# The query stage of a two-block kernel: raw tiles and a division by the norm afterwards

## The chip, the cores and the metric

The kernel runs on one core of one Trainium2 chip. The metric is the device time of one execution in microseconds, measured on the same chip for both kernels; a profiled execution has a time of its own. An engine is a queue of instructions that runs in its own order: TensorE (products, PE in the profile), VectorE (DVE), ScalarE (ACT), GpSimd (POOL, here only DMA issue) and SyncE (SP, here only the loads of the weight stream).

## The reference, cut to what matters

Two transformer blocks over 256 tokens of width 1024 in float32. The first has two layers (sparse attention, a short convolution, an MLP). The second has one layer: two kinds of attention, then a retrieval of experts by product keys. The change touches the step between them, in these lines:

```python
def rms_norm(x, g):
    xf = x.astype(jnp.float32)
    y = xf * lax.rsqrt(jnp.mean(xf * xf, axis=-1, keepdims=True) + EPS)
    return (y * g.astype(jnp.float32)).astype(x.dtype)

def modulate(h, shift, scale):
    return h * (1.0 + scale[:, None, :]) + shift[:, None, :]

        x = x + gate1[:, None, :] * (mixed @ w_out[layer])
        h2 = modulate(rms_norm(x, norm2_g[layer]), shift2, scale2)
        x = x + gate2[:, None, :] * peer(h2, w_query[layer], sub_keys[layer],
                                          u_experts[layer], v_experts[layer])

    # in peer, for the tokens xc of h2:
        qh = (xc @ w_query).reshape(PEER_CHUNK, PEER_HEADS, PEER_QDIM)
        s1 = jnp.einsum('thd,hnd->thn', qh[..., :PEER_HALF], sub_keys[:, 0]).astype(jnp.float32)
        s2 = jnp.einsum('thd,hnd->thn', qh[..., PEER_HALF:], sub_keys[:, 1]).astype(jnp.float32)
        # top 16 of each, top 16 of their sums, softmax, then u and v of the chosen experts
```

For one token, h2 = r * (a * x) + shift2, where r is one number of the token (the reciprocal root of its mean square) and a = gain * (1 + scale2) and shift2 are vectors over the 1024 features. So a query is r * ((a * x) @ w_query) + shift2 @ w_query. The expert stage, which follows, needs h2 itself.

## The kernel before, in words

**Weights.** All weights come as one stream of pieces of [128, 1024] float32, 512 KB each, in the order of use, through a ring of four slots (`RING`). A piece is split in two numbers, w_hi (ScalarE, `split_hi`, line 185) and w_lo (VectorE, `split_lo`, line 190). Each product is then three TensorE instructions (`mm3`, lines 213 to 215): hi by hi, lo by hi, hi by lo. `next_piece` starts each piece, and first issues the split of the piece three ahead (`AHEAD`): w_hi waits until that piece has landed and until the slot's old piece has been used, w_lo waits for w_hi, the load of the next piece into the raw slot (SyncE, line 563) waits for w_lo. `piece_b` runs one piece of 8 feature tiles against the 256 tokens: 24 products of 256 columns. TensorE waits in `next_piece` for w_lo of its piece.

**Marks.** `PE`, `AC` and `VE` are helpers (class `Line`) for the queues of TensorE, ScalarE and VectorE: `VE.go(marks, method, ...)` waits for the marks, issues the instruction (line 88) and returns its mark. Each engine runs strictly what was written for it, in the order of the Python program, so an instruction that waits holds all behind it on its engine. `free[b]` holds the marks after which PSUM bank b may be written again, and `take(b)` waits for them on TensorE.

**Before the query stage.** The output product of the attention (`out_part`) fills banks 0 to 3: 2 token tiles (tt) by 2 column halves (n). `add_out(tt, n)` multiplies a bank by the gate and adds it to x, two VectorE instructions; `square_of` squares the chunk on ScalarE and sums it. `token_roots` makes the reciprocal root of each token by a chain of 15 small VectorE instructions, `diagonals` puts the roots on the diagonals of two 128x128 matrices. `keep_clock` issues products whose result nobody reads. `modulated_to_u` multiplies x by the diagonals on TensorE (line 1169), which turns and divides it in one step (32 products), and then makes the eight feature tiles of h2: scale and shift to hT, alternately on ScalarE and VectorE, u_hi on ScalarE, u_lo on VectorE.

**The query stage.** 16 pieces of w_query. The first two run tile by tile as the tiles become ready (`two_pieces`, lines 229 to 241), the other 14 in pairs through `piece_b`, each pair in a half of one bank (4, 5 or 6); ScalarE copies them to qhT, which lies in the big buffer Z. `key_scores(h)` makes 8 small products (line 1576) of the queries 2h and 2h + 1 with the sub-keys, and VectorE copies them out. The last three come together at the end. Then the expert stages start: 256 pieces, the first 64 beside the choice of the experts, which is VectorE's. x is written to memory (x_parked) before Z takes its place.

**Layer boundary.** Between the two layers of the first block the same thing is done in another way: `added_and_turned` turns x undivided (line 366), lowers the eight tiles with the gain alone, and the root is applied later.

Of the kernel before, what the change touches and what calls it, by code (L numbers as in the profile page):

```python
# [8 lines left out]
F32 = mybir.dt.float32  # L9
# [8 lines left out]
P = 128  # L18
# [31 lines left out]
U_SHIFT, U_REST = 56, 8  # L50
N_LAYER = 59 + 2 * KH
# [42 lines left out]
def build(nc, stream, x_in, gains2, gain_cols, conv_w, w_ada, b_ada, c_cols, kept_in, rope_in, na_mask_in,  # L94
          t5_in, t5_hot, rpb_pad, sinks, sub_keys, gain_out, out):
    ctx = ExitStack()
    with ctx:
        def sb(c, name, shape, dt=F32):
            return c.enter_context(nc.sbuf_tensor(name, shape, dt))
# [117 lines left out]
        def piece_b(o, rhs_hi, rhs_lo, kt=KD, parts=1, last=False, ready=None):  # L217

            s = next_piece(last)
            for part in range(parts):  # L220
                for k in range(kt):
                    if ready is not None:
                        PE.wait(*ready[k])
                    col = (part * kt + k) * P
                    i = mm3(o[part], w_hi[:, s, col:col + P], w_lo[:, s, col:col + P],
                            rhs_hi[:, k, :], rhs_lo[:, k, :], k == 0, k == kt - 1)
            return used(i)
# [292 lines left out]
        ph1a = ph1.enter_context(ExitStack())  # L520
        rope_t = sb(ph1a, "rope", [P, 2, T])
# [4 lines left out]
        gate = sb(ph1a, "gate", [P, 2 * KD, T])  # L526
# [10 lines left out]
        o_hi, o_lo = sb(ph1a, "o_hi", [P, KW, T], F32R), sb(ph1a, "o_lo", [P, KW, T], F32R)  # L537
        y_hi, y_lo = sb(ph1a, "y_hi", [P, KW, T], F32R), sb(ph1a, "y_lo", [P, KW, T], F32R)
# [545 lines left out]
        bias_a, bias_b = sb(ph1b, "bias_a", [P, H, BIAS_W]), sb(ph1b, "bias_b", [P, H, BIAS_W])  # L1084
        na_mask = sb(ph1b, "na_mask", [P, GRID_W])
        sink = sb(ph1b, "sink", [P, H])
# [6 lines left out]
        og, junk = sb(ph1b, "og", [P, 2, W]), sb(ph1b, "junk", [P, 2, W])  # L1093

# [53 lines left out]
        def diagonals(r):  # L1148
            for tt in range(NT):
                m = VE.go((r, (s_kept, 16)), V.tensor_scalar, diag[:, tt, :], ident, st[:, 3, tt:tt + 1], None, ALU.mult)  # L1150
                got["diag", tt] = m

# [352 lines left out]
        square_of(x, 5, x_marks, 0, 1)  # L1505
        PE.wait(*got["mixed", 1, 1])
# [6 lines left out]
        split_lo(c + KW)  # L1513
        for n in range(2):
# [25 lines left out]
        qhT = Z[:, 0:N_QUERY * T].rearrange("p (f t) -> p f t", t=T)  # L1540
        skT = Z[:, N_QUERY * T:N_QUERY * (T + PK)].rearrange("p (f n) -> p f n", n=PK)
# [17 lines left out]
        AC.wait((s_park, 16))  # L1559
        VE.wait((s_park, 16))  # L1560
        take(4), take(5)
        pair = two_pieces([bank[4][:, 0:T], bank[5][:, 0:T]], h2_ready)
        for f in range(2):
            m = AC.go((pair[f],), S.activation, qhT[:, f, :], bank[4 + f][:, 0:T], ACT.Copy)
            free[4 + f] = (m,)
        S.dma_start(skT, sub_keys).then_inc(s_sk, 16)
        q_there = [m]

        def key_scores(h):
# [3 lines left out]
            PE.wait(q_there[h], (s_sk, 16))  # L1573
# [9 lines left out]
        for f in range(2, N_QUERY, 2):  # L1583
            b = 4 + (f // 2) % 2 if f > 2 else 6
            take(b)
            piece_b([bank[b][:, 0:T]], *U)
# [4 lines left out]
            q_there.append(m)  # L1591
            if 2 < f < N_QUERY - 2:
                key_scores(f // 2 - 2)
        key_scores(PH - 3)
        key_scores(PH - 2)
        m = key_scores(PH - 1)
# [485 lines left out]
```

## Time and profile before

| | us |
|---|---|
| median of 3 runs | 1728.52 |
| lowest and highest | 1727.76, 1728.98 |
| the profiled execution's own time | 1727.02 |
| its span | 1725.7 |
| TensorE busy | 1700.7 (99%) |
| VectorE busy | 1328.3 (77%) |
| ScalarE busy | 926.5 (54%) |

The place of the change lies at 877 to 939 us of the span. The mean granted clock of TensorE over the span is 0.997 of full speed. A TensorE row shows when a product was issued; its duration is longer than the distance to the next, because products are pipelined, so costs are read from start to start. Rows of VectorE and ScalarE overlap by about 0.1 us with their neighbours when nothing is waited for.

### The profile page before, as it was taken

What the parts mean: (1) busy time and instruction counts of PE and PEld (TensorE: products, weight loads), DVE (VectorE), ACT (ScalarE), POOL (GpSimd) and SP (SyncE); (2) the same over time, 40 slices, a digit from 0 to 9 for tenths busy, and PEclk for the clock granted to TensorE, in tenths of its full rate; (3) what the DMA queues carried; (4) which work ended last, traced back from release to release, by engine and by line L of the source; (5) the groups of instructions that cost most, each with busy time, mean ns of one, the idle gap of its engine ahead of it and who ended that gap; (6) DMA issues with size and microseconds to landing.
All of it is one profiled execution on the core that took longest, in us unless ns stands there. A gap on an engine that the chain in (4) does not pass through costs nothing.

```text
span 1725.7 us, 33390 instructions
## 1 busy us (share of the span) xinstructions
PE 1700.7 (99%) x11670; PEld 1567.1 (91%) x11670; DVE 1328.3 (77%) x2382; ACT 926.5 (54%) x1647; POOL 63.3 (4%) x112
## 2 busy tenths in 40 slices
PE   9999999999999999999999999999999999999997
PEld 8899899989999899999889999999999988888886
DVE  7986778778976788877775999978888766666666
ACT  5454544455454544455554555577777655444553
POOL 0000001000000122100000000000000000000000
PEclk9999999999999999999999999999999999999999
DMA  6555687755445699744344555554444455555554
GB/s 233 174 187 205 209 294 270 250 174 171 159 160 168 221 329 327 238 153 140 123 167 152 173 170 179 182 171 141 141 138 144 141 191 193 194 194 194 191 192 152
DMA packets 90122, 327.30 MB, mean 190 GB/s; under 512 B 11000, under 2 KB 11176, under 8 KB 89584
## 3 DMA queue, kind: packets, MB, share of 16 engines
q1 hardware_dynamic: 79056, 286.45, 48.8%
q0 software_dynamic: 9712, 34.36, 6.0%
q10 hardware_dynamic: 1264, 5.24, 0.8%
q8 instruction: 62, 1.02, 0.2%
q14 instruction: 28, 0.23, 0.0%
HBM read 323.88 MB, written 6.09 MB: 191 GB/s over the span
## 4 chain that ended last, share of the span: by engine, by line
PE 80%; DVE 16%; issue 2%; ACT 1%; DMA 0%; DVEq 0%; ACTq 0%
PE bank L213 24%; PE bank L215 24%; PE bank L214 24%; DVE Z L88 6%; DVE w_lo L190 5%; PE bank L1772 3%; PE bank L284 1%; DVE yc L88 1%; PE bank L276 1%; PE bank L1313 1%; PE bank L484 1%; DVE work L88 1%; DVE rot L88 1%; DVE top L88 1%; PE bank L1264 0%
## 5 line engine op out<-in xcount | busy, mean ns | idle before, releaser
L190 DVE TENSOR_TENSOR w_lo<-raw,w_hi 128x1024 fp32r<-128x1024 f32 x544 | 658.0, 1220 | 154.1 <-ACT w_hi L185 153.3
L185 ACT ACTIVATE w_hi<-raw 128x1024 fp32r<-128x1024 f32 x544 | 572.5, 1054 | 229.2 <-PE bank L215 162.4
L213 PE MATMUL bank<-u_hi,w_hi 128*128 128x256 f32 x2400 | 686.2, 286 | 3.7 <-DVE w_lo L190 3.0
L214 PE MATMUL bank<-u_lo,w_hi 128*128 128x256 f32 x2400 | 674.7, 281 | 0.0
L215 PE MATMUL bank<-u_hi,w_lo 128*128 128x256 f32 x2400 | 674.7, 281 | 0.0
L213 PEld LDWEIGHTS bank<-u_hi,w_hi 128*128 128x128 f32 x2400 | 453.0, 189 | 12.8 <-DVE w_lo L190 4.3
L214 PEld LDWEIGHTS bank<-u_lo,w_hi 128*128 128x128 f32 x2400 | 453.2, 189 | 2.3
L215 PEld LDWEIGHTS bank<-u_hi,w_lo 128*128 128x128 f32 x2400 | 452.9, 189 | 0.0
L215 PE MATMUL bank<-w_hi,a_lo 128*128 128x512 f32 x744 | 290.6, 391 | 0.0
L214 PE MATMUL bank<-w_lo,a_hi 128*128 128x512 f32 x744 | 290.4, 390 | 0.0
L213 PE MATMUL bank<-w_hi,a_hi 128*128 128x512 f32 x744 | 289.9, 390 | 0.0
L215 PEld LDWEIGHTS bank<-w_hi,a_lo 128*128 128x128 f32 x744 | 139.6, 188 | 29.4
L213 PEld LDWEIGHTS bank<-w_hi,a_hi 128*128 128x128 f32 x744 | 139.9, 188 | 27.9 <-issue 0.2
L214 PEld LDWEIGHTS bank<-w_lo,a_hi 128*128 128x128 f32 x744 | 139.6, 188 | 28.1
L1861 ACT ACTIVATE a_hi<-Z 128x256 fp32r (+1 forms) x126 | 52.7, 418 | 169.0 <-PE bank L215 167.2
L1863 DVE TENSOR_TENSOR a_lo<-Z,a_hi 128x256 fp32r<-128x256 f32 x126 | 53.6, 425 | 81.6 <-ACT a_hi L1861 81.6
L1761 ACT ACTIVATE rows_a<-rows_a,sel 128x128 f32<-128x128 f32 x256 | 81.2, 391 | 0.0
L1745 DVE TENSOR_TENSOR rows_a<-kept,sel 128x512 f32<-128x512 f32 x64 | 44.2, 691 | 34.5 <-PE bank L1772 34.5
L962 ACT ACTIVATE qT<-bank 128x256 f32<-128x256 f32 x64 | 24.6, 384 | 82.5 <-PE bank L215 82.3
L1608 ACT ACTIVATE Z<-bank 128x256 f32 (+1 forms) x68 | 26.1, 384 | 76.8 <-PE bank L215 76.7
L971 DVE CAST a_hi<-qT 128x256 fp32r<-128x256 f32 x60 | 18.1, 301 | 48.4 <-PE bank L215 47.3
L997 DVE SCALAR_TENSOR_TENSOR space<-gate,c_tmp,space 128x1024 f32 x42 | 53.7, 1280 | 0.4
(286 smaller groups left out, 1710.6 us busy)
## 6 DMA issues: line engine op xcount, KB each, us to landing
raw<-stream SPq DMA_DIRECT2D x544, 512.0 KB, 3.3
gate<-w_ada POOLq DMA_DIRECT2D x48, 512.0 KB, 6.0
t_rows<-t_by_distance POOLq DMA_DIRECT2D x8, 256.0 KB, 3.1
rpb_rows<-rpb_pad POOLq DMA_DIRECT2D x8, 224.0 KB, 4.1
bias_b<-rpb_rows POOLq DMA_DIRECT2D x16, 96.0 KB, 6.3
bias_a<-t_rows POOLq DMA_DIRECT2D x1, 1536.0 KB, 13.1
x<-x_in ACTq DMA_DIRECT2D x2, 512.0 KB, 5.5
gains_b<-gains POOLq DMA_DIRECT2D x1, 1024.0 KB, 8.7
```

Source lines behind the costliest of these rows:

```text
L88: return self.done(method(*args, **kw))
L185: nc.scalar.activation(w_hi[:, s, :], raw[:, s, :], ACT.Copy).then_inc(s_hi, 1)
L190: nc.vector.tensor_tensor(w_lo[:, s, :], raw[:, s, :], w_hi[:, s, :].bitcast(F32), ALU.subtract).then_inc(s_split, 1)
L213: M.matmul(o, lh, rh, start=start, stop=False, skip_group_check=True)
L214: M.matmul(o, lh, rl, start=False, stop=False, skip_group_check=True)
L215: return M.matmul(o, ll, rh, start=False, stop=stop, skip_group_check=True)
L997: nc.vector.scalar_tensor_tensor(total, ada_raw[:, k % ADA_RING, :], c_act[:, k:k + 1], total, ALU.mult, ALU.add).then_inc(s_ada, 1)
L1745: return V.tensor_tensor(out, iota.unsqueeze(1).to_broadcast([P, GROUP, P]), values.unsqueeze(2).to_broadcast([P, GROUP, P]), ALU.is_equal)
L1761: i = S.activation(rows_a[:, q, e, :], rows_a[:, q, e, :], ACT.Copy, scale=share[:, e:e + 1])
L1772: i = M.matmul(bank[6 + q][:, e * P:(e + 1) * P], rows_a[:, q, e, :], rows_b[q][:, e, :].bitcast(F32), start=True, stop=True, skip_group_c ...
L1861: S.activation(hi[:, q, :], zj, ACT.Copy).then_inc(s_ah, 1)
L1863: V.tensor_tensor(lo[:, q, :], zj, hi[:, q, :].bitcast(F32), ALU.subtract).then_inc(s_al, 1)
```

## The change

The tiles of a * x (`raw_u_hi`, `raw_u_lo`) are made from x before its norm is known, as at the layer boundary, with two columns more: both hold shift2, so that a product of 258 columns gives the query of all tokens and, in column 256, shift2 @ w_query. The first ten query pieces run on these. Each result is then multiplied by a row of the roots (`token_row`, made by two small products with the diagonals) and the shift's part is added. x is turned by plain transposes, eight of them between the halves of the last output products, with each pair of feature tiles in one of the banks 4 to 7. The eight tiles of h2 are made from the same banks by `tile_fixed`, between the steps of pieces 6 to 9. Pieces 10 to 15 run on h2 as before. The filler products, the scaling products, `two_pieces` and `modulated_to_u` are not used here any more. The squares of the last two chunks and the waits for the parking of x move behind; the bias tables give their place to the raw tiles.

```diff
         def piece_b(o, rhs_hi, rhs_lo, kt=KD, parts=1, last=False, ready=None, order=None):
             s = next_piece(last)
+            order = order or tuple(range(kt))
             for part in range(parts):
-                for k in range(kt):
+                for k in order:
...
+        def turn_tile(k, tt, marks, turned):
+            b, col = turn_place(k)          # bank 4 + k // 2, half k % 2
+            if tt == 0 and k % 2 == 0:
+                take(b)
+            PE.wait(marks[tt][k // 4], (s_kept, 16))
+            i = M.transpose(bank[b][:, col + tt * P:col + (tt + 1) * P], x[:, tt, k * P:(k + 1) * P], ident)
+            if tt == NT - 1:
+                turned[k] = PE.done(i)
+
+        def shift_columns(hi, lo, j, scaled):
+            src = acol[:, 2 * j, :].unsqueeze(2).to_broadcast([P, KD, 2])
+            m1 = AC.go((scaled,), S.activation, hi[:, :, T:T + 2], src, ACT.Copy)
+            return m1, VE.go((m1, scaled), V.tensor_tensor, lo[:, :, T:T + 2], src, hi[:, :, T:T + 2].bitcast(F32),
+                             ALU.subtract)
+
+        LOWER_ORDER = (0, 2, 1, 3, 4, 6, 5, 7)
+
+        def lower_scaled(k, hi, lo, j, scaled, turned):
+            b, col = turn_place(k)
+            src, gain, t = bank[b][:, col:col + T], acol[:, 2 * j + 1, k:k + 1], turned[k | 1]
+            m1 = AC.go((t, scaled, *(free[b] if k % 2 else ())), S.activation, hi[:, k, 0:T], src, ACT.Copy, scale=gain)
+            m = VE.go((m1, t, scaled), V.scalar_tensor_tensor, lo[:, k, 0:T], src, gain, hi[:, k, 0:T].bitcast(F32),
+                      ALU.mult, ALU.subtract)
+            free[b] = (m1, m)
+            return m1, m
+
+        def roots_as_row(b):
+            take(b)
+            PE.wait(got["diag", 0], got["diag", 1])
+            for tt in range(NT):
+                i = M.matmul(bank[b][:, tt * P:(tt + 1) * P], one[:, 0:1].to_broadcast([P, P]), diag[:, tt, :],
+                             start=True, stop=True, skip_group_check=True)
+            m = AC.go((PE.done(i),), S.activation, token_row[:, :], bank[b][:, 0:T], ACT.Copy)
+            free[b] = (m,)
+            return m
+
+        def rooted_and_shifted(b, dst, n, done, row):
+            m1 = AC.go((done,), S.activation, side_sum[:, n:n + 1], bank[b][:, T:T + 1], ACT.Copy)
+            m = VE.go((done, row, m1), V.tensor_tensor, dst, bank[b][:, 0:T], token_row[:, :], ALU.mult)
+            free[b] = (m, m1)
+            return AC.go((m, m1), S.activation, dst, dst, ACT.Identity, bias=side_sum[:, n:n + 1])
...
         split_hi(c + KW)
         split_lo(c + KW)
+        for k in range(KD):
+            turn_tile(k, 0, x_marks, turned2)
         for n in range(2):
...
             add_out(1, n)
+        for k in range(KD):
+            turn_tile(k, 1, x_marks, turned2)
+        raw_ready = {k: lower_scaled(k, *raw2, 1, scaled, turned2) for k in LOWER_ORDER}
+        split_lo(c + KW + 1)
+        split(c + KW + 2)
+        for n in range(2):
             square_of(x, 5, x_marks, 1, n)
-        take(5)
-        keep_clock(5, 20)
         diagonals(token_roots(junk_mark[0]))
-        split_lo(c + KW + 1)
         S.dma_start(x_dram.rearrange("t p d -> p t d"), x[:, :, :]).then_inc(s_park, 16)
-        split_hi(c + KW + 2)
-        h2_ready = modulated_to_u(x, x_marks, scaled, 1, 1)
-        split_lo(c + KW + 2)
...
+        def raw_query(f, b):
+            take(b)
+            return piece_b([bank[b][:, 0:T + 2]], *RAW2, ready=raw_ready if f == 0 else None,
+                           order=LOWER_ORDER if f == 0 else None)
+
+        def query_fixed(f, b, m):
+            q_there[f] = rooted_and_shifted(b, qhT[:, f, :], f, m, row)
+
+        def tile_fixed(k):
+            b, col = turn_place(k)
+            src, h = bank[b][:, col:col + T], hT[:, k % 4, :]
+            m = VE.go((row, turned2[k | 1]), V.scalar_tensor_tensor, h, src, acol[:, 3, k:k + 1], token_row[:, :],
+                      ALU.mult, ALU.mult)
+            free[b] = (m,)
+            m1 = AC.go((m,), S.activation, u_hi[:, k, :], h, ACT.Identity, bias=acol[:, 2, k:k + 1])
+            h2_ready[k] = (m1, VE.go((m, m1), V.scalar_tensor_tensor, u_lo[:, k, :], h, acol[:, 2, k:k + 1],
+                                     u_hi[:, k, :].bitcast(F32), ALU.add, ALU.subtract))
...
+        PE.wait(*shifts2)
+        m = raw_query(0, 0)
+        side_mark = AC.go((m,), S.activation, side_sum[:, 0:1], bank[0][:, T:T + 1], ACT.Copy)
+        first_there = AC.go((m,), S.activation, qhT[:, 0, :], bank[0][:, 0:T], ACT.Copy)
+        free[0] = (first_there,)
+        S.dma_start(skT, sub_keys).then_inc(s_sk, 16)
+        asked = {f: raw_query(f, f) for f in (1, 2)}
+        row = roots_as_row(3)
+        asked[3] = raw_query(3, 0)
+        m = VE.go((first_there, row), V.tensor_tensor, qhT[:, 0, :], qhT[:, 0, :], token_row[:, :], ALU.mult)
+        q_there[0] = AC.go((m, side_mark), S.activation, qhT[:, 0, :], qhT[:, 0, :], ACT.Identity,
+                           bias=side_sum[:, 0:1])
+        query_fixed(1, 1, asked[1])
+        asked[4] = raw_query(4, 3)
+        query_fixed(2, 2, asked[2])
+        query_fixed(3, 0, asked[3])
+        asked[5] = raw_query(5, 1)
+        query_fixed(4, 3, asked[4])
+        query_fixed(5, 1, asked[5])
+        asked[6] = raw_query(6, 2)
+        tile_fixed(0)
+        query_fixed(6, 2, asked[6])
+        asked[7] = raw_query(7, 3)
+        tile_fixed(1)
+        query_fixed(7, 3, asked[7])
+        key_scores(0)
+        asked[8] = raw_query(8, 2)
+        tile_fixed(2)
+        tile_fixed(3)
+        query_fixed(8, 2, asked[8])
+        key_scores(1)
+        asked[9] = raw_query(9, 3)
+        tile_fixed(4)
+        tile_fixed(5)
+        query_fixed(9, 3, asked[9])
+        tile_fixed(6)
+        tile_fixed(7)
+        for f in range(N_RAW, N_QUERY, 2):      # N_RAW = 10
+            b = 4 + (f // 2) % 2
             take(b)
-            piece_b([bank[b][:, 0:T]], *U)
+            piece_b([bank[b][:, 0:T]], *U, ready=h2_ready if f == N_RAW else None)
             m = piece_b([bank[b][:, T:2 * T]], *U)
...
+            key_scores(f // 2 - 3)
+        for h in range(PH - 3, PH):
+            m = key_scores(h)
+        AC.wait((s_park, 16))
+        VE.wait((s_park, 16))
```

## Rows read from the trace of the kernel before

**Rows 1.** The page, parts 1 and 4: busy time, and the chain by engine.
```profile
PE 1700.7 (99%) x11670; PEld 1567.1 (91%) x11670; DVE 1328.3 (77%) x2382; ACT 926.5 (54%) x1647; POOL 63.3 (4%) x112
PE 80%; DVE 16%; issue 2%; ACT 1%; DMA 0%; DVEq 0%; ACTq 0%
```

**Rows 2.** Timeline of TensorE, 876 to 887: start us, us, engine, line, operation, count, idle before.
```profile
877.44 0.39 PE L215 MATMUL bank<-w_hi,mx_lo 128*128 128x512 f32 x1
...
877.66 4.54 PE L276 MATMUL bank<-one_r 128*128 128x512 f32 x20
...
882.45 3.84 PE L1169 MATMUL bank<-space,x 128*128 128x128 f32 x32 [0.25 <-DVE space L88]
...
886.04 0.36 PE L213 MATMUL bank<-u_hi,w_hi 128*128 128x256 f32 x1
```

**Rows 3.** Busy time by stretch: us, each engine, PEclk, DMA share, GB/s.
```profile
910.00:936.00 26.00, 26.00 (x224) 26.00 (x224) 12.54 (x12) 10.35 (x12) 0.00 (x0) 1.00 0.48 163
```

**Rows 4.** Timeline of VectorE and ScalarE, 878 to 883.
```profile
878.59 0.69 DVE L88 TENSOR_TENSOR x<-x,hT 128x512 f32<-128x512 f32 x1
...
879.31 0.63 ACT L88 ACTIVATE space<-x 128x512 f32<-128x512 f32 x1 [0.67 <-DVE x L88]
...
880.07 0.16 DVE L88 SCALAR_TENSOR_TENSOR st<-st 128x2 f32<-128x2 f32 x1 [0.79 <-ACT space L88]
...
882.11 0.48 DVE L88 TENSOR_SCALAR space<-kept,st 128x128 f32<-128x128 f32 x2
```

**Rows 5.** Timeline, the first tile of h2: the three steps on two engines.
```profile
883.64 0.54 DVE L88 TENSOR_SCALAR hT<-bank,acol 128x256 f32<-128x256 f32 x1
884.21 0.42 ACT L88 ACTIVATE u_hi<-hT 128x256 fp32r<-128x256 f32 x1 [3.23 <-DVE hT L88]
...
884.73 0.43 DVE L88 TENSOR_TENSOR u_lo<-hT,u_hi 128x256 fp32r<-128x256 f32 x1 [0.55 <-ACT u_hi L88]
```

**Rows 6.** Timelines of TensorE, ScalarE and VectorE at the layer boundary, 383 to 388.
```profile
383.91 1.77 PE L366 MATMUL bank<-kept,x 128*128 128x128 f32 x12
...
384.22 3.02 ACT L88 ACTIVATE u_hi<-bank,kept 128x256 fp32r<-128x256 f32 x8 [1.51 <-PE bank L366]
...
384.78 3.21 DVE L88 SCALAR_TENSOR_TENSOR u_lo<-bank,kept,u_hi 128x256 fp32r<-128x256 f32 x8
```

**Rows 7.** Groups by form, whole span: count, busy us, mean ns, idle before.
```profile
L190 DVE TENSOR_TENSOR w_lo<-raw,w_hi 128x1024 fp32r<-128x1024 f32 x544 | 658.0, 1220 | 154.1 <-ACT w_hi L185 153.3 <-DVE Z L88 0.3
...
L965 DVE TENSOR_TENSOR qT<-qT,bank 128x256 f32<-128x256 f32 x64 | 26.5, 414 | 2.2 <-ACT qT L962 1.9
...
L88 DVE SCALAR_TENSOR_TENSOR u_lo<-bank,kept,u_hi 128x256 fp32r<-128x256 f32 x32 | 12.9, 475 | 0.0
...
L88 ACT ACTIVATE p<-p,rows 128x256 f32<-128x256 f32 x16 | 7.9, 496 | 1.1 <-DVE rows L88 1.1
```

**Rows 8.** Timeline of TensorE, the last pieces and key scores of the stage.
```profile
929.43 1.05 PE L1576 MATMUL bank<-Z 128*128 128x128 f32 x8
...
936.00 2.84 PE L1576 MATMUL bank<-Z 128*128 128x128 f32 x24
938.59 0.36 PE L213 MATMUL bank<-u_hi,w_hi 128*128 128x256 f32 x1
```

**Rows 9.** Timelines of VectorE and ScalarE, 890 to 900: splits of weights.
```profile
890.28 2.35 DVE L190 TENSOR_TENSOR w_lo<-raw,w_hi 128x1024 fp32r<-128x1024 f32 x2
...
895.65 1.06 ACT L185 ACTIVATE w_hi<-raw 128x1024 fp32r<-128x1024 f32 x1 [1.40 <-DMA raw<-stream]
...
899.42 1.06 ACT L185 ACTIVATE w_hi<-raw 128x1024 fp32r<-128x1024 f32 x1 [1.14 <-DMA raw<-stream]
```

**Rows 10.** Timeline of TensorE at 454, and busy time by stretch behind it.
```profile
453.99 0.72 PE L429 MATMUL bank<-kT,qT 64*128 64x128 f32 x8 [2.44 <-DVE qT L88]
...
455.00:457.00 2.00, 2.00 (x12) 2.00 (x11) 2.00 (x4) 0.00 (x0) 0.00 (x0) 0.50 0.33 106
457.00:459.00 2.00, 2.00 (x14) 2.00 (x13) 1.03 (x1) 0.00 (x0) 0.00 (x0) 0.66 0.90 289
```

More of the change, by code:

```diff
@@ L50 @@
 U_SHIFT, U_REST = 56, 8
+U_WIDE = T + 16
 N_LAYER = 59 + 2 * KH
@@ L215, in mm3, with piece_b @@
             return M.matmul(o, ll, rh, start=False, stop=stop, skip_group_check=True)
-        def piece_b(o, rhs_hi, rhs_lo, kt=KD, parts=1, last=False, ready=None):
+        def piece_b(o, rhs_hi, rhs_lo, kt=KD, parts=1, last=False, ready=None, order=None):
             s = next_piece(last)
+            order = order or tuple(range(kt))
             for part in range(parts):
-                for k in range(kt):
+                for k in order:
                     if ready is not None:
@@ L225, in piece_b @@
                     i = mm3(o[part], w_hi[:, s, col:col + P], w_lo[:, s, col:col + P],
-                            rhs_hi[:, k, :], rhs_lo[:, k, :], k == 0, k == kt - 1)
+                            rhs_hi[:, k, :], rhs_lo[:, k, :], k == order[0], k == order[-1])
             return used(i)
@@ L520, in build @@
         ph1a = ph1.enter_context(ExitStack())
+        gate = sb(ph1a, "gate", [P, 2 * KD, T])
+        o_hi, o_lo = sb(ph1a, "o_hi", [P, KW, T], F32R), sb(ph1a, "o_lo", [P, KW, T], F32R)
+        y_hi, y_lo = sb(ph1a, "y_hi", [P, KW, T], F32R), sb(ph1a, "y_lo", [P, KW, T], F32R)
         rope_t = sb(ph1a, "rope", [P, 2, T])
@@ L1093, in build @@
         og, junk = sb(ph1b, "og", [P, 2, W]), sb(ph1b, "junk", [P, 2, W])
+        token_row, side_sum = sb(ph1b, "token_row", [P, T]), sb(ph1b, "side_sum", [P, 3 * KD])
+        na_mask = sb(ph1b, "na_mask", [P, GRID_W])
+        sink = sb(ph1b, "sink", [P, H])
+        ph1c = ph1b.enter_context(ExitStack())
+        bias_a, bias_b = sb(ph1c, "bias_a", [P, H, BIAS_W]), sb(ph1c, "bias_b", [P, H, BIAS_W])
         G.wait_ge(s_naw, 16 * 8)
@@ L1505, in build @@
         square_of(x, 5, x_marks, 0, 1)
+        ph1c.close()
+        raw2 = [sb(ph1c, name, [P, KD, U_WIDE], F32R) for name in ("raw_u_hi", "raw_u_lo")]
+        shifts2 = shift_columns(*raw2, 1, scaled)
+        turned2 = {}
         PE.wait(*got["mixed", 1, 1])
@@ L1557, in build @@
         smx = tail(2 * NT * PH).rearrange("p (a n) -> p a n", a=2)
[L1559 to L1567, printed above, removed]
+        RAW2 = tuple(a[:, :, 0:T + 2] for a in raw2)
+        N_RAW = 10
+        U = (u_hi, u_lo)
+        q_there, h2_ready = {}, {}
+        def raw_query(f, b):
[13 more added lines that the diff above has]
+                                     u_hi[:, k, :].bitcast(F32), ALU.add, ALU.subtract))
         def key_scores(h):
@@ L1572, in key_scores @@
             take(b)
-            PE.wait(q_there[h], (s_sk, 16))
+            PE.wait(q_there[2 * h + 1], (s_sk, 16))
             for tt in range(NT):
@@ L1581, in key_scores @@
             return m
-        for f in range(2, N_QUERY, 2):
-            b = 4 + (f // 2) % 2 if f > 2 else 6
+        PE.wait(*shifts2)
[37 more added lines that the diff above has]
+            b = 4 + (f // 2) % 2
             take(b)
-            piece_b([bank[b][:, 0:T]], *U)
+            piece_b([bank[b][:, 0:T]], *U, ready=h2_ready if f == N_RAW else None)
             m = piece_b([bank[b][:, T:2 * T]], *U)
```

19 lines of the change are left out of this document (5 added, 14 removed).

## The prediction

> **What bounds the kernel now.** I read four views, in this order. The page first: TensorE is busy for 99% of the span, and it holds 80% of the chain that ended last [rows 1], so a change saves time only where it takes work or idle time off TensorE's queue. Then TensorE's timeline at the place of the edit. The last output product starts at 877.44 and the first query product at 886.04 [rows 2]. Between them lie only the 20 filler products and the 32 scaling products: 8.6 us in which the stream of useful products stands. Then the busy time by stretch: from 910 to 936 TensorE is busy for 26.00 of 26.00 us [rows 3], and the other engines show gaps. The expert stages behind are TensorE's as well, so what the query stage wins or loses arrives at the end unchanged. Last, the timelines of VectorE and ScalarE, which show what fills the 8.6 us: the add of the last chunk of x (878.59), the square (879.31), the root chain from 880.07, the two diagonals from 882.11 [rows 4], the scaling products, and the first tile (883.64 to 885.16) [rows 5].
>
> All times below are on the clock of that profiled execution: span 1725.7 us, its own time 1727.02. The median of the runs is 1728.52, so I add 1.5 us at the end.
>
> **The front: what is gained.** The root leaves the path to the first query product. Eight transposes go between the halves of the last output products. The trace has 12 in 1.77 us [rows 6] and 32 of the same size in 3.84 [rows 2], 0.12 to 0.15 each: 0.9 to 1.2 us, of which I take 0.9. The last output product then ends 0.9 later, and so does the second step of its add: 879.28 + 0.9 gives 880.15. The eight remaining transposes are two waits of four; the last four follow that add, 0.45 us. The lowering of a raw tile (ScalarE copy with gain, VectorE subtract) is the work of the layer boundary, where eight tiles took 3.02 and 3.21 us, 0.39 a tile [rows 6]. Here two tiles share a bank and the second must wait for VectorE's read of the first, so I count 0.46 a tile. VectorE runs 880.1 to 883.8, TensorE takes piece 0 behind it from 880.6 to 884.2.
>
> Piece 1 needs its w_lo, which now stands on VectorE behind the eight tiles: 883.7 + 1.22 [rows 7], start 885.0, a stall of 0.8. Then pieces 1 and 2 run to 890.7, two small products of the row of roots cost 0.25, and piece 3 starts at 890.95. Squares, roots, diagonals and w_lo of pieces 2 to 4 fill VectorE until 890.7 and are ahead of need. In the kernel before, a piece costs 2.85 (two pieces and a key score take 936.00 - 929.43 = 6.57, and three key scores 2.59, 0.86 each [rows 8]), so piece 3 started at 886.04 + 3 x 2.85 = 894.6. The front therefore gains 3.6 us and not 8.6: transposes and lowering take the rest. The columns added for the shift: a 512-column product is issued every 4.54/20 = 0.227 us [rows 2], a 256-column one every 2.85/24 = 0.119; by that slope two columns cost 0.9 ns, 240 of them 0.2 us. The trace shows no width between 256 and 512. Its bounds are nothing and the price of a 512-column product (a rival below).
>
> **The middle: what is lost.** From piece 3 on, the new work is written into the in-order queues of ScalarE and VectorE between the weight splits, and nearly every step waits for the other engine. Going through the queues in the order of the program: raw_query(f) first issues w_hi then w_lo of piece f + 3; then, for each query fixed, VectorE's multiply by token_row waits on ScalarE's one-column copy, and ScalarE's Identity waits on the multiply; for each tile, VectorE's multiply, ScalarE's u_hi, VectorE's u_lo, each waiting on the one before; and the next w_hi stands behind the last Identity. Prices:
> - split: 1.06 on ScalarE [rows 9], 1.22 on VectorE, less the overlap of neighbours (two w_lo in 2.35 [rows 9]): 2.2.
> - fixed query: multiply 0.41 [rows 7], Identity with a bias column from SBUF. This is not in the trace; nearest are the plain copy of the same size, 0.42 [rows 5], and the Exp with a bias column, 0.50 [rows 7]. I take 0.50, since it has the column. The one-column copy I put at 0.2 (0.42 for 256 columns and 0.63 for 512 [rows 4, 5] leave 0.21 at none); most of it lies beside w_lo. Together 0.95 to 1.0.
> - tile: multiply from PSUM 0.48 [rows 7], u_hi 0.50, u_lo 0.43 to 0.48, less 0.1 overlap plus two handoffs of 0.03 to 0.1 (884.18 to 884.21 and 884.63 to 884.73 [rows 5]): 1.4. The first tile of the kernel before took 1.52 for three such steps [rows 5].
>
> The Trainium skill (ScalarE: Activation LUTs, What ACT_TABLE_LOAD costs) says that each [128,1] pointer operand adds about 93 ns to an ACTIVATE. The 0.50 against 0.42 in the rows agrees; by the plain copy's price the sum below would be 1.4 us smaller.
>
> The chain begins with w_hi of piece 6. It waits for its raw tile, whose load starts when w_lo of piece 2 ends (886.0). At that time x_parked and sub_keys, 1 MB each, load too; in the kernel before, beside sub_keys alone, the loads started at 891.4 and 892.6 (w_lo until 892.63) were used at 895.65 and 899.42 [rows 9], 4.2 and 6.8 us later. I take 6.8: 892.9. With 4.2 or less, the row of roots (891.6) would decide, 1.3 earlier. From one w_hi to the next:
> - 6 to 7: split, first query fixed in two steps, query 1: 4.2 (897.1)
> - 7 to 8, 8 to 9: split and two queries, 4.2 each (905.5)
> - 9 to 10, 10 to 11: split, one tile, one query, 4.5 each (914.5)
> - 11 to 12: split, two tiles, one query, 6.0 (920.5)
> - 12 to the last u_lo: split, four tiles, one query, 8.45 (928.95)
>
> A piece costs TensorE 2.85, so it is held up throughout: piece 7 waits for bank 3 (query 4 fixed) until 903.9, piece 8 for bank 2 until 909.6, piece 9 for bank 3 until 914.1 and ends at 917.0. Piece 10 needs all eight tiles, and its last can start only at 929.0. TensorE stands for about 9.5 us there, and piece 10 ends at 929.35. Behind it: piece 11, a key score, four pieces with a key score between, four key scores, 5 x 2.85 + 6 x 0.86 = 19.4, to 948.8. Before, this point was 938.59 [rows 8]: 10.2 us later.
>
> **The clock.** After an idle stretch of 2.44 us at 451.5 to 453.99 the granted clock was 0.50 in 455 to 457 and 0.66 in 457 to 459, the lower level of 1.2 GHz [rows 10]: 2 x 0.50 + 2 x 0.34 = 1.7 us lost. In piece 10 the gaps between tiles are up to 4 us, and TensorE leaves it at the lower level; one such recovery then falls on the full stream of piece 11. I take 1.7, with 0 and 3.4 as ends. The shorter waits before pieces 7 to 9 may also cost clock, but there the two other engines decide, and it is hidden. The filler that is removed covered the 8.6 us; the new gap there is about 1.6 us, partly filled with transposes.
>
> Everything else I cost at nothing: x_parked is issued later, but waited for only behind the stage; the key scores of the first heads move later, and the copies of their results are counted as VectorE work beside ScalarE's; the two shift columns are made beside output products.
>
> **Sum:** 10.2 + 1.7 = 11.9 us later. 1727.02 + 11.9 = 1738.9, on the scale of the median 1740.4. Its own range: without clock loss, with the fast load and with the copy's price 11.9 - 1.7 - 1.3 - 1.4 = 7.5, so 1736; with 3.4 of clock and some 45 handoffs at 0.08 instead of 0.04, 11.9 + 1.7 + 1.8 = 15.4, so 1744.
>
> **Rivals.**
> - *The handoffs hide (not slower).* Counted by busy time alone, a raw piece asks 1.06 + 0.2 + 0.5 = 1.8 us of ScalarE and 1.22 + 0.41 = 1.6 of VectorE, less than 2.85, and VectorE's whole work from 889.5 on (nine w_lo, ten multiplies, sixteen tile steps, two copies of scores, 10.2 + 3.5 + 6.4 + 1.2 = 21.3 without waits) would end near 911. If the two run side by side, TensorE stays full to the end of piece 9 near 911, and only query 9 and the last two tiles (3.5 us against the 2.5 that piece 10 leaves them) hold it, 1.1. Then -3.6 + 0.2 + 1.1 = -2.3: 1726. For it: both engines show idle time. Against: the order of the queues, in which each step waits for the one just issued on the other engine. It decides wherever a split with its repairs takes under 2.85. Chance 0.11.
> - *The handoffs hide in part.* Queries keep up and only tiles 0 to 7 are serial, so the loss just eats the gain: within 3.5 us of before. 0.07.
> - *The raw products are slow.* 258 columns at the price of 512: 240 x 0.108 = 26 us more on TensorE, which takes over from the chain: piece 9 would end near 937 instead of 917, then 3.5 and 19.4 us, 961, or 22 us later: 1751. Nothing in the trace speaks for a step behind 256. 0.05.
> - *No clock loss*, or loads that land fast: 1737 to 1739, part of the forecast, which has 0.77 in all, near 0.7 of it in its own range.
>
> Faster, same and slower by 0.2% (3.5 us, about what these runs can tell from no change): the first rival gains 2.3 us and reaches 3.5 only with yet cheaper transposes: faster 0.06, same 0.12, slower 0.82. The range 1731 to 1744 leaves out the last rival, most of the first, and a little of the second.
>
> **What would show it.** First raw product at 880.6, piece 3 at about 891. A ladder in the timelines of ScalarE and VectorE in which one is idle while the other works, with w_hi every 4.2 us from 893, then 4.5 and 6. TensorE waiting for tiles in piece 10, the last at about 929, with the clock at 0.5. Products of 258 columns still 0.12 apart. The stage ending near 950. I am wrong if TensorE is full from 885 to 930, or if w_hi comes every 2.9.

## The result and the profile after

The changed kernel takes 1744.34 us (median of 4 runs, 1743.09 to 1745.18), the kernel before beside it 1728.75 (4 runs, 1727.76 to 1729.55). The ratio is 1.0091, 95% interval 1.0078 to 1.0104: 15.6 us slower. The forecast was 1740.4 with a range of 1731 to 1744: the sign and the ladder of handoffs were right, the size was 3.9 us short and lies just outside the range. The profiled execution of the changed kernel took 1744.12, its span 1742.8; its stage ends 16.8 us later than before, and its span is 17.1 longer. (That is more than 15.6, since the profiled execution of before lay 1.7 under its median and this one 0.2 under.)

TensorE's timeline, 872 to 893 (start, duration, engine, line, operation, count, idle before):

```profile
872.63 0.47 PE L214 MATMUL bank<-w_hi,mx_hi 128*128 128x512 f32 x1
...
875.50 1.03 PE L1166 MATMUL bank<-kept,x 128*128 128x128 f32 x8
876.29 0.48 PE L214 MATMUL bank<-w_hi,mx_hi 128*128 128x512 f32 x1
...
880.85 0.66 PE L1166 MATMUL bank<-kept,x 128*128 128x128 f32 x4 [0.75 <-DVE x L89]
881.34 0.36 PE L214 MATMUL bank<-raw_u_hi,w_hi 128*128 128x258 f32 x1
...
885.73 0.39 PE L214 MATMUL bank<-raw_u_hi,w_hi 128*128 128x258 f32 x1 [0.45 <-DVE w_lo L191]
...
891.59 0.61 PE L1194 MATMUL bank<-space,one 128*128 128x128 f32 x4
891.95 0.37 PE L214 MATMUL bank<-raw_u_hi,w_hi 128*128 128x258 f32 x1
892.15 0.28 PE L215 MATMUL bank<-raw_u_lo,w_hi 128*128 128x258 f32 x1
892.27 0.28 PE L216 MATMUL bank<-raw_u_hi,w_lo 128*128 128x258 f32 x1
```

This is the front, in place of the fillers and scaling products of [rows 2]. The first query product comes at 881.34 instead of 886.04, piece 1 stalls for 0.45 on its w_lo, and piece 3 starts at 891.95. Products of 258 columns are 0.12 apart, like those of 256. The row at 872.63 stands at 872.00 in the kernel before: this execution was 0.6 us late before any changed instruction.

The chain that ended last, 884 to 906 (start, duration, what). It leaves TensorE for the whole ladder (the row of w_hi steps up to piece 12 and the tiles behind it); over the span TensorE holds 76% of it, against 80% in [rows 1]:

```profile
884.54 2.28 DVE w_lo L191 x2
886.98 10.25 DMA raw<-stream
897.26 1.07 ACT w_hi L186
898.38 1.11 issue
899.49 0.43 DVE Z L89
899.94 0.51 ACT Z L89
900.61 0.44 DVE Z L89
901.09 0.39 issue
901.48 1.05 ACT w_hi L186
```

First a load of 10.25 us, then one step of the ladder in full: w_hi, w_lo, VectorE's multiply, ScalarE's Identity, the second multiply, the second Identity and the next w_hi. (The two "issue" rows are w_lo, on VectorE from 898.35 to 899.57, and the second Identity, on ScalarE from 901.07 to 901.58.) One engine works, the other waits. ScalarE's timeline has the w_hi of pieces 5 to 12 (the rows between them are left out):

```profile
891.18 1.06 ACT L186 ACTIVATE w_hi<-raw 128x1024 fp32r<-128x1024 f32 x1 [2.62 <-DMA raw<-stream]
...
897.26 1.06 ACT L186 ACTIVATE w_hi<-raw 128x1024 fp32r<-128x1024 f32 x1 [4.64 <-DMA raw<-stream]
...
901.48 1.04 ACT L186 ACTIVATE w_hi<-raw 128x1024 fp32r<-128x1024 f32 x1
...
905.70 1.04 ACT L186 ACTIVATE w_hi<-raw 128x1024 fp32r<-128x1024 f32 x1
...
909.91 1.04 ACT L186 ACTIVATE w_hi<-raw 128x1024 fp32r<-128x1024 f32 x1
...
914.53 1.04 ACT L186 ACTIVATE w_hi<-raw 128x1024 fp32r<-128x1024 f32 x1
...
919.14 1.04 ACT L186 ACTIVATE w_hi<-raw 128x1024 fp32r<-128x1024 f32 x1
...
925.28 1.04 ACT L186 ACTIVATE w_hi<-raw 128x1024 fp32r<-128x1024 f32 x1
```

From piece 6 on the distances are 4.22, 4.22, 4.21, 4.62, 4.61 and 6.14. TensorE's waits between 878 and 956 (line, who releases, us in total, times, longest):

```profile
PE bank L214 <- DVE Z L89: 6.5, 4, 3.1
PE bank L214 <- DVE u_lo L89: 6.4, 4, 4.0
PE bank L214 <- DVE hT L89: 1.5, 1, 1.5
```

And TensorE from tile 3 of piece 10 to the first expert piece:

```profile
924.65 0.36 PE L214 MATMUL bank<-u_hi,w_hi 128*128 128x256 f32 x1
...
929.25 0.36 PE L214 MATMUL bank<-u_hi,w_hi 128*128 128x256 f32 x1 [4.01 <-DVE u_lo L89]
...
934.16 0.55 PE L214 MATMUL bank<-u_hi,w_hi 128*128 128x256 f32 x1 [0.55 <-DVE u_lo L89]
...
951.92 3.73 PE L1652 MATMUL bank<-Z 128*128 128x128 f32 x32
955.41 0.36 PE L214 MATMUL bank<-u_hi,w_hi 128*128 128x256 f32 x1
```

The last tile comes at 934.16, and the stage ends at 955.41 against 938.59 [rows 8].

### The profile page after: what moved, and what is told of

It is laid out like the page before. It is cut to its first block, busy times and chain, and to the rows that moved or that the text cites. A ratio compares the mean times of both kernels' runs of the same rounds, so it can differ in the third digit from the quotient of the medians.

```text
span 1742.8 us, 33405 instructions
## 1 busy us (share of the span) xinstructions
PE 1702.5 (98%) x11638; PEld 1566.0 (90%) x11638; DVE 1337.7 (77%) x2405; ACT 931.0 (53%) x1668; POOL 63.3 (4%) x112
## 3 DMA queue, kind: packets, MB, share of 16 engines
q8 instruction: 62, 1.02, 0.2%
## 4 chain that ended last, share of the span: by engine, by line
PE 76%; DVE 17%; issue 3%; ACT 2%; DMA 2%; DVEq 0%; ACTq 0%; SPq 0%
PE bank L214 23%; PE bank L215 23%; PE bank L216 23%; DVE Z L89 6%; DVE w_lo L191 5%; PE bank L1885 3%; DMA raw<-stream 1%; ACT w_hi L186 1%; DVE yc L89 1%; PE bank L286 1%; PE bank L1367 1%; PE bank L486 1%; DVE work L89 1%; DVE rot L89 1%; DVE top L89 1%
## 5 line engine op out<-in xcount | busy, mean ns | idle before, releaser
L214 PE MATMUL bank<-u_hi,w_hi 128*128 128x256 f32 x2320 | 665.9, 287 | 11.6 <-DVE u_lo L89 6.9
L215 PE MATMUL bank<-u_lo,w_hi 128*128 128x256 f32 x2320 | 653.0, 281 | 0.0
L216 PE MATMUL bank<-u_hi,w_lo 128*128 128x256 f32 x2320 | 652.8, 281 | 0.0
L214 PEld LDWEIGHTS bank<-u_hi,w_hi 128*128 128x128 f32 x2320 | 438.5, 189 | 22.3 <-ACT u_hi L89 6.9
L215 PEld LDWEIGHTS bank<-u_lo,w_hi 128*128 128x128 f32 x2320 | 439.3, 189 | 2.2
L216 PEld LDWEIGHTS bank<-u_hi,w_lo 128*128 128x128 f32 x2320 | 438.6, 189 | 0.0
```

Source lines behind the costliest of these rows:

```text
L214: M.matmul(o, lh, rh, start=start, stop=False, skip_group_check=True)
L215: M.matmul(o, lh, rl, start=False, stop=False, skip_group_check=True)
L216: return M.matmul(o, ll, rh, start=False, stop=stop, skip_group_check=True)
```

## The experiments

All were run beside the kernel before, but not all on the same chip: its medians beside them are 1728.33 to 1728.87, so up to 0.5 us of a difference between two experiments can be the chip's. Executions of kernels with equal code ahead of the stage enter it up to 1.8 us apart, so positions are compared by their distance from the w_hi of piece 2, at 883.92 in the changed kernel and at 883.1 to 884.9 in experiments 1 to 6.

**1 to 3. The two transfers.** The changed kernel issues the parking of x and the load of sub_keys at 885.6 and 886.2, just ahead of the load of piece 6.

```diff
-        S.dma_start(x_dram.rearrange(...), x[:, :, :]).then_inc(s_park, 16)   # behind the diagonals
-        S.dma_start(skT, sub_keys).then_inc(s_sk, 16)                         # behind raw piece 0
         asked[4] = raw_query(4, 3)
+        S.dma_start(skT, sub_keys).then_inc(s_sk, 16)                         # e1, e2
...
         asked[6] = raw_query(6, 2)
+        S.dma_start(x_dram.rearrange(...), x[:, :, :]).then_inc(s_park, 16)   # e1, e3
```

> Edit: the load of sub_keys (1 MB) is issued behind the start of raw piece 4, and the parking of x (1 MB) behind the start of raw piece 6, instead of beside the first raw pieces; nothing else is changed. My theory: of the 5 us that the prediction missed, nearly 4 come from w_hi of piece 6, whose load took 10.3 us from issue to landing beside these two transfers. Without them it lands in under 5 us, w_hi 6 starts near 892 instead of 897.3, the same ladder follows 5 us earlier, the expert stage starts near 950.4 instead of 955.4 and the time is about 1739.3, 5 us less than the changed kernel. Rival A: the weight load is slow by itself, or held by the work before it on SyncE: w_hi 6 stays near 897 and the time at 1744. Rival B: the handoffs behind it decide (tiles, queries), so that the earlier start is lost in piece 10: under 1.5 us gained.

> Edit: only the load of sub_keys is issued later, behind the start of raw piece 4. My theory: x_parked still shares the bandwidth with the load of piece 5 and 6, so w_hi 6 starts between 893.5 and 895.5, 2 to 4 us of the 5 are gained, time near 1741.5. If sub_keys alone were the cause, the time would be that of both loads later, near 1739; if the parking alone were, 1744.

> Edit: only the parking of x is issued later, behind the start of raw piece 6. My theory: it gains the other part, w_hi 6 between 893.5 and 895.5, time near 1741.5; the two single edits add up to about that of both together (5 us), perhaps to a little more, since with one transfer gone the other ends sooner. If the parking, which writes to memory, takes nothing from loads: 1744.

Measured: both later 1740.55 us (1740.38 to 1740.65), sub_keys later 1739.43 (1738.85 to 1739.49), parking later 1740.26 (1739.43 to 1741.22), so 3.8, 4.9 and 4.1 less than the changed kernel. From w_hi 2 to w_hi 6 it is 13.34 us in the changed kernel, and 8.59, 9.03 and 9.28 in these: 4.8, 4.3 and 4.1 less, and from w_hi 2 to the end of the stage 4.4, 3.9 and 3.7 less. The ladder behind is the same to 0.02 us a step (4.22, 4.22, 4.21 with both later). So the late load is the missing term, and rivals A and B are out. But the two edits do not add up, though I had expected them to; either alone is nearly enough. ScalarE's timeline with both later shows why:

```profile
890.15 1.06 ACT L186 ACTIVATE w_hi<-raw 128x1024 fp32r<-128x1024 f32 x1 [0.63 <-DMA raw<-stream]
893.20 0.39 ACT L89 ACTIVATE token_row<-bank 128x256 f32<-128x256 f32 x1 [1.98 <-PE bank L1194]
893.48 1.05 ACT L186 ACTIVATE w_hi<-raw 128x1024 fp32r<-128x1024 f32 x1
```

w_hi 6 (893.48) stands behind the copy of the row of roots, which waits for TensorE's small products. A load earlier than that is worth nothing, and removing either transfer gets the load in at about that time. (With the parking alone later it is the load of piece 5 that is late: its w_hi, at 892.79, holds the copy and then w_hi 6.)

One transfer less gains 4.1 us or more, though its 1 MB at the 400 GB/s or so of that stretch takes only 2.6. The bytes that the queues moved account for the rest. From 885.6 to the landing of piece 6 at 897.24 they are 4.06 MB: the two transfers with 2.10, and 1.95 of the stream, of which pieces 5 and 6 are 1.05. The other 0.9 belong to pieces 7 and 8, whose loads are issued at about 890.6 and 891.8, behind that of piece 6 but before it lands. With sub_keys later only 2.32 MB were moved up to the landing. That is 1.74 MB less, or 4.4 us at 398 GB/s. Why bytes of later loads move before the earlier load has landed, no run here shows.

**4. The order of the handoffs.**

```diff
-            return AC.go((m, m1), S.activation, dst, dst, ACT.Identity, bias=side_sum[:, n:n + 1])
+            return m, m1
+        def shifted(dst, n, marks):
+            return AC.go(marks, S.activation, dst, dst, ACT.Identity, bias=side_sum[:, n:n + 1])
...
         asked[5] = raw_query(5, 1)     # issues w_hi and w_lo of piece 8
+        late_shifts()                  # the Identities of the queries multiplied before it
```

> Edit: the order of ScalarE's queue alone. The Identity that adds the shift to each repaired query is issued behind the w_hi of the next piece instead of ahead of it. The number of instructions on every engine is unchanged. My theory: the ladder is made of handoffs between two queues in order, not of work; w_hi then no longer waits for VectorE's multiply, a step from one w_hi to the next falls from 4.2 to about 3.0 where only queries are repaired, and the whole is near 1734.5, 10 us less than the changed kernel. Rival (the work itself fills the two engines): w_hi to w_hi stays above 4 and the time stays at 1744.

Measured: 1735.61 us (1734.77 to 1737.33), 8.7 less than the changed kernel, with the same instructions in number and kind. ScalarE's timeline from w_hi 6 on:

```profile
896.90 1.06 ACT L186 ACTIVATE w_hi<-raw 128x1024 fp32r<-128x1024 f32 x1 [4.62 <-DMA raw<-stream]
...
897.98 1.06 ACT L186 ACTIVATE w_hi<-raw 128x1024 fp32r<-128x1024 f32 x1
...
900.51 1.06 ACT L186 ACTIVATE w_hi<-raw 128x1024 fp32r<-128x1024 f32 x1
...
903.20 1.06 ACT L186 ACTIVATE w_hi<-raw 128x1024 fp32r<-128x1024 f32 x1
```

The load is as late as before, but the steps are 1.08, 2.53 and 2.69 instead of 4.2. (The first is so short because the w_hi of piece 7 no longer waits for anything.) Where queries are repaired, the ladder is made of waiting and not of work. Where tiles are made, whose own handoffs this edit leaves as they were, the steps are 3.21, 3.21 and 5.11 instead of 4.62, 4.61 and 6.14.

**5. The clock.** TensorE's granted clock has two levels here, 1.00 (2.4 GHz) and 0.50 (1.2 GHz).

```diff
                 for k in order:
+                    if fill and k in fill:          # {4: 16, 5: 4, 6: 4, 7: 2} for piece 10
+                        take(0)
+                        keep_clock(0, fill[k])
                     if ready is not None:
```

> Edit: 26 products that nobody reads are put into piece 10 ahead of its tiles 4 to 7 (16, 4, 4 and 2), where TensorE waits for VectorE; they go to bank 0. Nothing else is changed. My theory: they fit into the waits (4 us ahead of tile 4, about 1.5 ahead of each of the others), keep the granted clock up, and the products behind the last tile are issued every 0.12 us instead of every 0.21 for the first 3 us: 1.3 us less, near 1743.0, visible in the trace as the distance from the last tile of piece 10 to the expert stage, 21.25 us in the changed kernel, 20.0 here. Rival (the clock is no term, or falls all the same): distance and time unchanged.

Measured: 1741.91 us (1741.64 to 1743.51). From the last tile of piece 10 to the expert stage the changed kernel takes 955.41 - 934.16 = 21.25 us, this one 954.95 - 935.06 = 19.89: 1.36 less. Busy time by stretch (the last columns are granted clock, DMA share, GB/s), first of the changed kernel, then with the fillers:

```profile
929.00:933.00 4.00, 1.93 (x8) 1.52 (x9) 2.59 (x7) 1.55 (x5) 0.00 (x0) 0.67 0.31 116
933.00:937.00 4.00, 3.45 (x16) 3.19 (x16) 2.38 (x3) 2.43 (x3) 0.00 (x0) 0.50 0.10 14
```

```profile
929.00:933.00 4.00, 3.42 (x17) 2.26 (x16) 2.18 (x6) 1.89 (x5) 0.00 (x0) 1.00 0.37 131
933.00:937.00 4.00, 3.10 (x22) 2.62 (x22) 2.65 (x5) 2.52 (x3) 0.00 (x0) 1.00 0.00 0
```

The granted clock was 0.50, the 1.2 GHz level, while TensorE took the last three tiles and the first products behind them; with the waits filled it stays at 1.00. The clock is a term of its own, 1.4 us. (The medians differ by 2.4 us, or 2.0 when each is taken against the kernel before beside it, and the intervals of the two ratios, 1.0078 to 1.0104 and 1.0066 to 1.0097, overlap: it is the trace and not the runs that shows this term.)

**6. Experiments 1 and 4 together.** The diff is that of both.

> Edit: the two edits together: the Identity of each query behind the next w_hi, and both transfers (sub_keys, parking of x) later. My theory: alone they gained 8.7 and 3.8 us. Together less than the sum: without the serial queries TensorE itself, at 2.85 us a piece, holds the ladder up to piece 9, so the earlier start helps only partly; arithmetic by the queues gives 12.6 in all, near 1731.7. What is left over the kernel before are the tiles of h2, each three steps between two queues, that TensorE waits for in piece 10. If the sum holds in full (12.5 to 13), the two are independent; if the loads give nothing more, 1735.5.

Measured: 1732.2 us (1731.0 to 1733.26, 8 runs), ratio to before 1.0026 (1.0015 to 1.0036): 12.1 less than the changed kernel. The sum of the two alone is 12.5, my estimate 12.6, so this doesn't tell whether they add up. It does tell what is left. TensorE's waits for tiles in piece 10 (three of four, 4.0 us in all):

```profile
916.00 0.36 PE L214 MATMUL bank<-u_hi,w_hi 128*128 128x256 f32 x1 [1.29 <-DVE u_lo L89]
...
919.38 0.55 PE L214 MATMUL bank<-u_hi,w_hi 128*128 128x256 f32 x1 [1.26 <-DVE u_lo L89]
...
920.90 0.55 PE L214 MATMUL bank<-u_hi,w_hi 128*128 128x256 f32 x1 [0.55 <-DVE u_lo L89]
```

**7 and 8. Every handoff one piece apart.** Both transfers stay later. `first_steps` issues VectorE's multiplies for queries and tiles, `second_steps` ScalarE's Identity and u_hi and then VectorE's u_lo:

```diff
         asked[5] = raw_query(5, 1)
-        query_fixed(4, 3, asked[4])
-        query_fixed(5, 1, asked[5])
+        second_steps()
+        first_steps(("q", 4), ("t", 2))        # e7; e8: ("q", 4), ("t", 3)
         asked[6] = raw_query(6, 2)
-        tile_fixed(0)
-        query_fixed(6, 2, asked[6])
+        second_steps()
+        first_steps(("q", 5), ("t", 3))        # e7; e8: ("q", 5), ("t", 4), ("t", 5)
```

> Edit: both transfers later, and every step that waits for the other engine is issued one piece later than the step it waits for: VectorE's multiplies for queries and tiles of piece f, then, behind the next piece's w_hi and w_lo, ScalarE's Identity and u_hi, then VectorE's u_lo. Tiles start at piece 3 instead of 6. The instructions are the same in kind and number. My theory: all of the loss is the order of the handoffs; TensorE stays full from piece 3 to 15 but for under 1.5 us, the stage ends near 936 against 938.6 in the kernel before, and the time is near 1726.5, 2 us under the kernel before. Rival A: the front gains less than 3.6 us and the time is that of before, 1728.7. Rival B: the work itself, not the order, fills the engines in piece 3 to 10: above 1731.

> Edit: as the one before, with eight raw pieces instead of ten: two queries less to repair, but all tiles needed two pieces (5.7 us) sooner. My theory: the repair work of queries 8 and 9 (1.9 us) and the earlier deadline cancel, since neither is on the path once the handoffs are apart: time equal to the ten-piece version within 1 us. Rival: the tiles become late and TensorE waits in piece 8, 2 us or more slower than with ten.

Measured, 11 runs each: ten pieces 1725.29 us (1723.95 to 1725.78), ratio to before 0.9984 (0.9975 to 0.9993); eight pieces 1724.62 (1723.64 to 1726.39), ratio 0.9981 (0.9972 to 0.9990). They are equal to each other within the noise and both under the kernel before, by 3.0 and 3.7 us. Busy time of the version with eight pieces from piece 3 to the end of the stage, and TensorE's waits between 878 and 956:

```profile
891.00:936.00 45.00, 45.00 (x386) 45.00 (x384) 30.92 (x46) 25.24 (x43) 0.00 (x0) 1.00 0.69 234
```

```profile
PE bank L1166 <- DVE x L89: 0.7, 1, 0.7
PE bank L214 <- DVE w_lo L191: 0.4, 1, 0.4
```

TensorE is full for 45.00 of 45.00 us at full clock, while VectorE (30.92) and ScalarE (25.24) do the work that was too slow in the changed kernel. Of TensorE's waits only those of the front are left. The stage ends at 935.92 against 938.59. The edit changes two things at once: the steps stand one piece apart, and the tiles start at piece 3 instead of 6. No run here separates them; experiment 4, where the queries' steps alone move, shows the first without the second.

**9. The transfers early again, handoffs apart.** This puts the two DMA lines of experiment 8 back to where the changed kernel has them.

> Edit: the eight-piece version with the steps one piece apart, but with both transfers (sub_keys, parking of x) where the changed kernel has them, ahead of the loads of pieces 5 and 6. My theory: the late load cost 4 us in the changed kernel only because every w_hi behind it was on a chain without slack. Here w_hi of piece 6 again waits for its load until about 897, and w_lo of piece 6 is there at about 899.5, while TensorE reaches piece 6 only at about 900.2; later steps have slack too. So the same wait costs under 1 us: 1724.6 to 1725.6. Rival (the transfers cost by themselves, wherever the handoffs are): about 4 us, 1728.7.

Measured: 1728.59 us (1727.0 to 1730.2, 11 runs), ratio to before 1.0002 (0.9993 to 1.0011), 4.0 more than with the transfers late (3.7 when each is taken against the kernel before beside it; 3.0 in the traces, from the first raw product to the end of the stage). I was wrong, the rival's number came out. The run also shows what order and tiles are worth without the transfers: it differs from the changed kernel in these and in two raw pieces less, and is 15.6 us faster when each is taken against the kernel before beside it. TensorE's timeline and then VectorE's show the way:

```profile
899.52 0.39 PE L214 MATMUL bank<-raw_u_hi,w_hi 128*128 128x258 f32 x1 [2.18 <-DVE Z L89]
```

```profile
897.57 1.22 DVE L191 TENSOR_TENSOR w_lo<-raw,w_hi 128x1024 fp32r<-128x1024 f32 x1 [4.64 <-ACT w_hi L186]
...
899.05 0.42 DVE L89 TENSOR_TENSOR Z<-bank,token_row 128x256 f32<-128x256 f32 x1
```

The weights of piece 6 were in time, as I had worked out. But VectorE's multiply of query 1, which frees bank 1 for piece 5, stands behind w_lo 6 and so behind the late load. I had followed the weights and not the banks.

**10. w_lo of piece 1 ahead of the last adds.**

```diff
             if not n:
                 split_hi(c + KW + 1)
+                split_lo(c + KW + 1)
             add_out(1, n)
...
-        split_lo(c + KW + 1)
```

> Edit: the eight-piece version, with w_lo of piece 1 put ahead of the last two adds instead of behind the lowering. My theory: the stall of 0.45 us ahead of piece 1 goes, but VectorE is then the later one ahead of the add, by 0.27 (its w_lo would end near 878.0, the add started at 877.73), and the first raw product comes that much later: 0.2 us gained, not to be told from nothing. Rival: the row of roots comes later or sooner with it and moves the stage by over 1 us.

Measured: 1724.45 us (1723.34 to 1725.28, 11 runs), ratio to before 0.9977 (0.9968 to 0.9986). Against experiment 8 this is not to be told from nothing in the runs. In the traces the stall ahead of piece 1 is gone, and from the first raw product to the end of the stage it is 54.11 us instead of 54.83: 0.7 gained, more than I had expected, since the first raw product comes hardly later. It has the lowest time and the lowest ratio of all versions, 4.1 us under the kernel before.

**11. The bank of experiment 9.**

```diff
+        first_steps(("q", 0), ("q", 1))
         asked[3] = raw_query(3, 0)     # issues w_hi and w_lo of piece 6
-        first_steps(("q", 0), ("q", 1), ("t", 0))
+        first_steps(("t", 0))
```

> The eight-piece version with both transfers early cost 4 us in the runs (3.1 in the two profiled executions) where I expected under 1. Its trace shows TensorE waiting 2.18 us ahead of piece 5 for VectorE's multiply of query 1, which frees bank 1 and stands behind w_lo of piece 6 in VectorE's queue. Edit: the multiplies of queries 0 and 1 are issued ahead of w_hi and w_lo of piece 6 instead of behind them; nothing else. My theory now: the late load reached TensorE through the bank and not through the weights. The 2.2 us go, and most of the 0.9 behind them, and the time is near 1725.5. Rival A (the weights themselves are late, or other repairs behind w_lo 6): TensorE waits as long at piece 6, and the time stays at 1728.6. Rival B (the transfers slow something else, such as the clock or the products): no wait in the trace and still 1728.6.

Measured: 1728.02 us (1726.63 to 1728.91, 11 runs), ratio to before 0.9994 (0.9985 to 1.0003). That overlaps with experiment 9, and most of the loss is still there. TensorE's timeline:

```profile
902.50 0.39 PE L214 MATMUL bank<-raw_u_hi,w_hi 128*128 128x258 f32 x1 [1.02 <-DVE Z L89]
905.87 0.39 PE L214 MATMUL bank<-raw_u_hi,w_hi 128*128 128x258 f32 x1 [0.23 <-DVE Z L89]
```

Piece 5 no longer waits, but piece 6 does, 1.02 us, for the multiply of query 2, which stands behind w_lo 7. TensorE is busy for 43.33 of the 45 us from 891 to 936, against 42.52 in experiment 9: 0.8 us of its 2.5 us of waits are gone. From the first raw product to the end of the stage it is 57.32 us, against 57.85 in experiment 9 and 54.83 in experiment 8, so 0.5 of 3.0. My theory had the way right (the bank and not the weights) and the gain wrong: the wait moved on to the next bank, as in rival A with other repairs. Here the late load delays every bank whose repair stands behind its w_lo in VectorE's queue. What makes up the rest of the 3.0 was not tested.

## Why the prediction was short, step by step

- **The front** (gain 3.6): piece 3 at 891.95 - 0.6 for the late entry, against the 894.6 worked out for before, is 3.3. (The trace of before agrees with the 894.6: its key score behind piece 5 starts at 903.16, three pieces of 2.85 later.) The eight transposes delay the next product from 875.50 to 876.29, 0.8; the first raw product was forecast for 880.6 and came at 881.34, or 880.7 without the entry. Right to 0.3.
- **The columns**: no step at 258. That rival is out.
- **The load of piece 6**: the step that failed. It set w_hi 6 at 892.9, and w_hi 6 came at 897.26. The prediction took 6.8 us from issue to landing, from the kernel before, where sub_keys alone was under way, and it named the parking of x beside it without a price. Measured are 10.25, 3.4 more, from an issue 0.35 later than forecast. The stretch of the changed kernel in which it waits, busy time as above:

```profile
889.00:897.00 8.00, 8.00 (x69) 8.00 (x69) 3.72 (x5) 1.44 (x2) 0.00 (x0) 1.00 1.01 398
```

The DMA engines are full (share 1.01) at 398 GB/s for 8 us. The bytes could have warned, but not with the whole size: 1 + 1 MB and the 0.5 MB loads of pieces 5 and 6 are 3.1 MB, 7.9 us at that rate. That is 1.1 more than the 6.8 taken and still 2.4 short. With the 0.9 MB of pieces 7 and 8 that moved before the landing it is 4.06 MB, 10.2 us.

The Trainium skill (DMA: Bandwidth & Descriptors, Queues, rings and completion order) says that a DMA engine takes turns between queues, packet by packet. The trace agrees where both queues have work. From 892 to 894 (queue, packets, MB, share of the engines; q1 is the weight stream, q10 the transfers, at that time sub_keys):

```profile
q10 hardware_dynamic: 73, 0.60, 70.5%
q1 hardware_dynamic: 64, 0.26, 31.8%
```

The numbers of packets are nearly equal, but those of sub_keys are twice as large, 8 KB against 4, and the stream gets a third of the bytes. From 888 to 890, beside the parking with its 4 KB packets, it had half (98 packets with 0.40 MB against 96 with 0.39). Taking turns doesn't explain that from 891 to 892 the stream moved only 4 packets. Experiments 1 to 3 show that the late load is worth the 4 us.

- **The ladder** (36.05 from w_hi 6 to the last u_lo): 934.03 - 897.26 = 36.8. Right to 0.7. A step with two queries was forecast at 4.2 and is 4.22; the steps with tiles are each 0.1 longer than forecast, and the last, with four tiles, 8.75 instead of 8.45. The Identity with a bias column took 0.51 where I took 0.50 and the plain copy has 0.42 [rows 5]; experiment 4 shows that its place in the queue and not its length makes the cost.
- **The end** (from the last u_lo: 21.5 with 1.7 of clock): 955.41 - 934.03 = 21.4. Right; the clock alone was taken as 1.7 and is 1.36.
- Sum in the traces: 11.9 + 0.6 (entry) + 0.35 + 3.4 (load) + 0.7 - 0.1 = 16.85, measured 16.8. The entry is chance of this execution and no step of the prediction.
- **The rival in which the handoffs hide** is true of the work and false of the order: experiments 7 and 8 have all of it beside TensorE, at 1724.6 to 1725.3 where the rival said 1726 (with both transfers late; with them early, in experiment 9, 1728.6). What my range left out was a transfer. It reached up by the clock and the handoffs and had nothing for a load slower than the nearest row.

## What to carry to other kernels

Between two in-order queues, a result and the step that needs it from the other engine belong one unit of the main stream apart: the same instructions cost 15.6 us in one order and, with two transfers placed later and the tiles started earlier, gained 3.0 in another (experiment 7). Before a transfer is moved ahead of a load that a chain waits for, add up the bytes in flight, those of loads issued before it lands too, against the rate that the trace shows at full DMA share, and take a row with fewer transfers as the lower end, not as the value. When a wait is judged harmless, follow every buffer that is freed behind it as well as the data.

## What the runs showed that I had not expected

- With both 1 MB transfers under way, w_hi 6 came 4.8 us later than the next limit (the row of roots) allows. With only the parking under way it came 0.4 later, held by its own load; with only sub_keys 0.7, held by the load of piece 5. Neither edit by itself would have shown what the other transfer costs.
- The load wait passes to TensorE by way of PSUM banks even where the weights have slack: 4.0 us in the runs and 3.0 in the traces, of which moving two multiplies returned 0.6 in the runs, within the spread, and 0.5 in the traces.
- TensorE's waits in piece 10 (4.01, 0.94, 0.89 and 0.55 us, with the three products of one tile between them) went with a granted clock that fell to 0.50 at about 930.4, in the second of them, and came back at about 937. With 26 unread products in these waits it stayed at 1.00.
